# Layer-norm roots and inverses taken on four tokens per partition, and spread to the channels by TensorE

## The reference, cut to what matters

```python
def layer_norm(x, g, b):
    mu = jnp.mean(xf, axis=-1, keepdims=True)
    var = jnp.mean(jnp.square(xf - mu), axis=-1, keepdims=True)
    y = (xf - mu) * lax.rsqrt(var + EPS)
    return y * g + b

z = rms_norm(x, norm1_g) @ w_in          # 12 chunks of 128 columns
y_pool, s_pool = pool_mix(u_pool, ...)   # window means, then a 128x128 product per group
h = depthwise_conv(a * sigmoid(gate)) + conv_dw_b
y_conv = swish(layer_norm(h, ln_g, ln_b))
x = x + concat(y_pool, y_conv) @ w_out + b_out
x = x + hier_moe(rms_norm(x, norm2_g))   # 32 experts, top 2 of a group
```

## Time and profile before

| | us |
|---|---|
| median of 3 runs | 1005.97 |
| lowest and highest | 1005.02, 1008.71 |
| the profiled execution's own time | 1007.59 |
| its span | 1005.6 |
| PE busy in the span | 926.5 |
| DVE busy | 844.0 |
| ACT busy | 584.8 |

### The profile page before, as it was taken

One profiled execution on the slowest core, in us unless ns is written; L12 is line 12 of the kernel. 1 busy time (PEld: TensorE's weight loads), 2 busy tenths in 40 slices (PEclk: granted clock), 3 DMA queues, 4 the chain that ended last, 5 costly groups with the idle time before them and its releaser, 6 DMA issues.

```text
span 1005.6 us, 14019 instructions
## 1 busy us (share of the span) xinstructions
PE 926.5 (92%) x4691; PEld 791.8 (79%) x4691; DVE 844.0 (84%) x972; ACT 584.8 (58%) x560; POOL 165.1 (16%) x201
## 2 busy tenths in 40 slices
PE   5999999968999988999999999999999999999920
PEld 5999988857888787788888888888888888888710
DVE  6488997897678767989989899898989989898858
ACT  7311101385322254778878787887778778787514
POOL 1000000000000022242222222222212222221100
PEclk9999999999999979999999999999999999999965
DMA  9321241321332258899999999999999999999897
GB/s 284 114 64 42 66 130 54 135 88 63 137 114 105 95 193 320 315 388 386 379 396 369 387 382 381 397 374 398 391 390 387 391 399 375 399 390 382 325 310 273
DMA packets 66986, 275.69 MB, mean 274 GB/s; under 512 B 11615, under 2 KB 26591, under 8 KB 42377
## 3 DMA queue, kind: packets, MB, share of 16 engines
q1 hardware_dynamic: 57161, 257.41, 67.9%
q0 software_dynamic: 9792, 17.85, 4.7%
HBM read 259.33 MB, written 31.38 MB: 289 GB/s over the span
## 4 chain that ended last, share of the span: by engine, by line
PE 86%; DVE 7%; issue 2%; DMA 2%; ACT 2%; SPq 0%; POOLq 0%; POOL 0%; DVEq 0%; ACTq 0%
PE ps L1193 11%; PE ps L1195 11%; PE ps L1194 11%; PE ps L1212 6%; PE ps L1210 6%; PE ps L1211 6%; PE ps L924 5%; PE ps L925 5%; PE ps L926 5%; PE ps L968 3%; PE ps L1082 3%; PE ps L1083 3%; PE ps L1084 3%; PE ps L1165 3%; DVE big L1718 2%
## 5 line engine op out<-in xcount | busy, mean ns | idle before, releaser
L1718 DVE TENSOR_TENSOR big<-arena,big 128x2048 fp32r<-128x2048 f32 x128 | 286.9, 2283 | 0.0
L815 ACT ACTIVATE big<-arena 128x2048 fp32r<-128x2048 f32 x128 | 237.9, 1908 | 1.8 <-PE ps L1195 1.4
L1193 PE MATMUL ps<-big,ring 128*128 128x512 f32 x508 | 201.6, 397 | 2.8 <-DVE big L1718 2.8
L1195 PE MATMUL ps<-big,ring 128*128 128x512 f32 x508 | 198.7, 391 | 0.0
L1194 PE MATMUL ps<-big,ring 128*128 128x512 f32 x508 | 198.3, 390 | 0.0
L1718 DVE TENSOR_TENSOR slot_tail<-arena,slot_tail 128x2048 fp32r<-128x2048 f32 x62 | 139.0, 2283 | 0.0
L815 ACT ACTIVATE slot_tail<-arena 128x2048 fp32r<-128x2048 f32 x62 | 115.5, 1918 | 0.2 <-DVE eob L1694 0.2
L1193 PEld LDWEIGHTS ps<-big,ring 128*128 128x128 f32 x508 | 95.7, 188 | 22.3 <-DVE big L1718 3.7
L1195 PEld LDWEIGHTS ps<-big,ring 128*128 128x128 f32 x508 | 95.8, 188 | 20.5
L1194 PEld LDWEIGHTS ps<-big,ring 128*128 128x128 f32 x508 | 95.8, 189 | 18.9
L1210 PE MATMUL ps<-slot_tail,hTr 128*128 128x512 f32 x248 | 99.2, 400 | 0.0
(11 more groups left out here) (269 smaller groups left out, 1424.7 us busy)
## 6 DMA issues: line engine op xcount, KB each, us to landing
arena<-in_w_eg SPq DMA_DIRECT2D x64, 1024.0 KB, 7.8
arena<-in_w_eu SPq DMA_DIRECT2D x64, 1024.0 KB, 8.7
arena<-in_w_ed SPq DMA_DIRECT2D x64, 1024.0 KB, 9.2
arena<-in_x_prompt SPq DMA_DIRECT2D x16, 512.0 KB, 4.3
arena<-y_scratch SPq DMA_DIRECT2D x16, 512.0 KB, 8.2
arena<-in_w_in SPq DMA_DIRECT2D x12, 512.0 KB, 3.7
arena<-in_conv_band SPq DMA_DIRECT2D x8, 576.0 KB, 4.2
arena<-in_w_out SPq DMA_DIRECT2D x8, 512.0 KB, 5.2
```

The costliest lines, as they stand in the source:

```text
L815: act.activation(we_h[n % SLOTS], raw[n % RAWS], ACT.Copy).then_inc(high_done, 1)
L1193: pe.matmul(out, part_h[b][:, k, :], wh[:, i, :], start=(k == 0), stop=False)
L1195: ins = pe.matmul(out, part_l[b][:, k, :], wh[:, i, :], start=False, stop=(k == KD - 1))
L1718: dve.tensor_tensor(we_l[n % SLOTS], raw[n % RAWS], we_h[n % SLOTS].bitcast(F32), ALU.subtract).then_inc(low_done, 1)
```

## The change

For blocks 0 and 1 the variance, root and inverse are no longer held in 128 identical rows of 512 tokens, but as a 128x4 table: token q x 128 + p in partition p, column q.

- `ln_variance(n)`: four matmuls with the squares as the stationary operand and one column of `mean_w` as the moving one, instead of one matmul over 512 columns.
- `ln_deviation(n)`: a root over 128x4 into `stat_tok`. For n = 1 it waits for `lnrs_done` instead of `nrm_done`.
- A new `ln_inverse(n)` on DVE: a reciprocal over 128x4, a wait for it, and a product of the identity with the four inverses, which gives four 128x128 diagonals side by side (`diag`, 128x512).
- A new `ln_spread(n)` on PE: `ones` times `diag`, one matmul over 512 columns, which leaves the inverses in all partitions of PSUM bank 7. `ln_normal(n)` loses its reciprocal and multiplies from there.
- The engines' orders change: see the diff and the rows below. Block 2 keeps its form; its reciprocal has a function of its own, directly ahead of `ln_normal(2)`.

```diff
+        diag = r_p[:, 0:BANK].rearrange("p (q t) -> p q t", q=BANK // P)
+        tok_sd, tok_rs = stat_tok[:, 0:BANK // P], stat_tok[:, BANK // P:2 * BANK // P]
...
+        inv_ps = [banks(7, 1), banks(7, 1), None]
...
                 act.wait_ge(var_done, n + 1)
                 if n == 1:
-                    act.wait_ge(nrm_done, 1)
-                act.activation(ln_sd[n], var_ps[n][:, 0:w], ACT.Sqrt, bias=eps[:, :]).then_inc(lnsd_done, 1)
+                    act.wait_ge(lnrs_done, 1)
+                out = ln_sd[n] if n == 2 else tok_sd
+                act.activation(out, var_ps[n] if n < 2 else var_ps[n][:, 0:w], ACT.Sqrt, bias=eps[:, :]).then_inc(lnsd_done, 1)
...
             pooled(1)
-            ln_deviation(1)
+            state_rows(1)
             wo_high(0)
             pooled(2)
+            ln_deviation(1)
             ln_square(2)
             wo_high(1)
+            pooled(3)
             wo_high(2)
-            state_rows(1)
-            pooled(3)
             wo_high(3)
...
             def ln_variance(n):
                 w = BLOCKS[n][1]
                 pe.wait_ge(sqs_done, n + 1)
+                if n < 2:
+                    for q in range(w // P):
+                        ins = pe.matmul(var_ps[n][:, q:q + 1], sq[n][:, 0, q * P:(q + 1) * P], mean_w[:, 0:1], start=True,
+                                        stop=True)
+                    ins.then_inc(var_done, 1)
+                    return
...
+            def ln_spread(n):
+
+                pe.wait_ge(lnrs_done, n + 1)
+                pe.matmul(inv_ps[n], ones[:, :], diag.rearrange("p q t -> p (q t)"), start=True, stop=True).then_inc(inv_done, 1)
...
                     pool_lin_product(0)
-
+                    ln_spread(0)
+
+            pe.wait_ge(u_done, NG)
+            pe.wait_ge(nrm_done, 1)
+            turn_state(1)
             pool_lin_product(1)
-            pe.wait_ge(lnsd_done, 1)
+            pe.wait_ge(st_done, 2)
             ln_variance(1)
-            pe.wait_ge(u_done, NG)
             pool_lin_product(2)
             pe.wait_ge(cen_done, 2)
             ln_mean(2)
-            pe.wait_ge(lnsd_done, 2)
-            turn_state(1)
+            ln_spread(1)
             pool_lin_product(3)
...
+            def ln_inverse(n):
+                w = BLOCKS[n][1]
+                dve.wait_ge(lnsd_done, n + 1)
+                if n == 2:
+                    dve.reciprocal(ln_sd[n], ln_sd[n]).then_inc(lnrs_done, 1)
+                    return
+                dve.reciprocal(tok_rs, tok_sd).then_inc(inv_step, 1)
+                dve.wait_ge(inv_step, n + 1)
+                dve.tensor_tensor(diag, ident[:, :].unsqueeze(1).to_broadcast([P, w // P, P]),
+                                  tok_rs.unsqueeze(2).to_broadcast([P, w // P, P]), ALU.mult).then_inc(lnrs_done, 1)
...
             windows(2)
+            ln_inverse(0)
             ln_center(1)
             ln_normal(0)
             windows(1)
             ln_square_sum(1)
             windows(0)
+            ln_inverse(1)
             ln_center(2)
```

More of the change, by code:

```diff
@@ L162, in trunk_kernel @@
                     for i in range(len(PHASED))]
-        ln_sd = [r_p[:, 0:BANK], r_p[:, 0:BANK], r_p[:, BANK:BANK + DEC]]
+        stat_tok = sb("stat_tok", [P, 2 * BANK // P])
+        ln_sd = [None, None, r_p[:, BANK:BANK + DEC]]
+        diag = r_p[:, 0:BANK].rearrange("p (q t) -> p q t", q=BANK // P)
+        tok_sd, tok_rs = stat_tok[:, 0:BANK // P], stat_tok[:, BANK // P:2 * BANK // P]
         sq_at = BANK + DEC
@@ L270, in trunk_kernel @@
         mean_ps = [banks(6, 1), banks(6, 1), banks(6, 1)[:, 0:DEC]]
-        var_ps = [banks(7, 1), banks(7, 1), banks(6, 1)[:, DEC:2 * DEC]]
+        var_ps = [banks(7, 1)[:, 0:BANK // P], banks(7, 1)[:, 0:BANK // P], banks(6, 1)[:, DEC:2 * DEC]]
+        inv_ps = [banks(7, 1), banks(7, 1), None]
         out_ps = [banks(2, 2), banks(4, 2)]
@@ L324, in trunk_kernel @@
         cur_seen, placed = sem("cur_seen"), sem("placed")
+        inv_done, inv_step = sem("inv_done"), sem("inv_step")
         def x_rows(t):
@@ L1094, in turn_hm @@
                 else:
-                    pe.wait_ge(st_done, 2)
+                    pe.wait_ge(nrm_done, 2)
                     pe.wait_ge(lnsd_done, 3)
@@ L1433, in ln_center @@
                     [P, len(PHASED), w // PH, PH]), ALU.subtract).then_inc(cen_done, 1)
+            def ln_inverse(n):
[8 more added lines that the diff above has]
+                                  tok_rs.unsqueeze(2).to_broadcast([P, w // P, P]), ALU.mult).then_inc(lnrs_done, 1)
             def ln_normal(n):
                 w = BLOCKS[n][1]
-                dve.wait_ge(lnsd_done, n + 1)
-                dve.reciprocal(ln_sd[n], ln_sd[n]).then_inc(lnrs_done, 1)
-                dve.wait_ge(lnrs_done, n + 1)
+                inverse = ln_sd[n] if n == 2 else inv_ps[n]
+                if n == 2:
+                    dve.wait_ge(lnrs_done, n + 1)
+                else:
+                    dve.wait_ge(inv_done, n + 1)
                 dve.wait_ge(cen_done, n + 1)
                 tapped, phased = mixed(n)
-                dve.tensor_tensor(tapped, tapped, ln_sd[n].unsqueeze(1).to_broadcast([P, NTAP, w]), ALU.mult)
-                dve.tensor_tensor(phased, phased, by_phase(ln_sd[n]).unsqueeze(1).to_broadcast(
+                dve.tensor_tensor(tapped, tapped, inverse.unsqueeze(1).to_broadcast([P, NTAP, w]), ALU.mult)
+                dve.tensor_tensor(phased, phased, by_phase(inverse).unsqueeze(1).to_broadcast(
                     [P, len(PHASED), w // PH, PH]), ALU.mult).then_inc(nrm_done, 1)
@@ L1617, in _ @@
             ln_normal(1)
+            ln_inverse(2)
             ln_normal(2)
```

## The result

The changed kernel takes 1016.5 us, the median of 4 runs (1015.75 to 1020.76). Beside it the kernel before took 1006.43 us (4 runs, 1005.02 to 1008.71). The ratio is 1.0104, with an interval of 1.0074 to 1.0133: **slower by about 10 us**, with 1015.4 predicted. The profiled execution took 1016.42 us at a span of 1014.6, against 1007.6 and 1005.6 before, so the two profiles differ by 9.0 us and the medians by 10.1.

A forecast was written before the change was run, and what follows sets the result against it. The prediction took PE, 86% of the chain, as the bound, with the starts of chunk 11 and `out_proj(0)` deciding. 1.4 + 6.3 + 1.7 = 9.4 us on a median of 1005.97 gave 1015.4, range 1010.5 to 1019.0.

The forecast's parts named there:

- Chunk 11: Block 0: root, inverse and spread stand ahead of this chunk on PE, which starts at 200.1, 1.4 us later.
- The walk through block 1: Queues between 211 and 226: DVE waits 6.65 us for ACT's late root; delays `out_proj(0)` by 6.3 us.
- The clock: PE's 3.75 us idle gap puts the second spread and part of the last pooling product at 1.2 GHz: 1.7 us.
- Rival 1: Clock stays at 2.4 GHz after PE's gap: plus 7.7 us, 1013.7; chance 23%.
- `out_proj(0)` begins at half speed before and after, which cancels: At the start of `out_proj(0)`: the same low clock in both kernels, so no difference in time.
- the sum of 9.4: Whole kernel: 1.4 + 6.3 + 1.7 = 9.4 us slower, 1015.4 for the median.
- rival 3: `out_proj(0)` finds the clock high, giving back 2.5 us, perhaps another 1.5: 1010.5 to 1011.5; chance 8%.
- Rival 2: Clock also low under transposes and products behind two earlier PE gaps: some 5 us more, 1020.5; chance 6%.
- The table load: Ahead of block 1's root on ACT: 1.28 us load counted; about 1.4 us drain by the skill's rule left out.
- Rival 5: Broadcast operands as slow as the 3.34 us reciprocal: 2.65 us more in each block, 1020.7; chance 4%.
- Rival 4: DVE is the true limit, so the cheaper reciprocals save up to 4.9 us: 1001; chance 7%.
- What the second reciprocal gives back: nothing: `ln_normal(1)` loses 3.35 us, but ACT's Silus must wait for block 2's root behind `out_proj(0)`: no gain.

The follow-up runs named there:

- the old order: Changed kernel with ACT and PE in the order of the kernel before, the spread of block 1 behind the last pooling product: 1008.81 us.
- the earlier root: Changed kernel with one call moved: ACT takes the root of block 1 right behind the state's eviction: 1011.82 us.
- block 1 alone: Changed kernel with block 0 back in its old form, block 1 in the new form with the changed orders: 1016.89 us.
- the gap filled: Changed kernel plus 30 unused transposes of the identity on PE ahead of the second spread: 1016.48 us.
- the new order: The reordered kernel with its 28 transposes, block 1 in the new form, its spread inside `out_proj(0)`, block 0 in the old form: 1003.66 us.
- the repetition: The changed kernel run again, unaltered, beside other experiments: 1018.21 us, ratio 1.0124.
- the second set: A later group of experiments, measured against 1006.53 us for the kernel before (23 runs).
- the reordered kernel: Kernel before, arithmetic kept, block 1's variance moved into `out_proj(0)`, its root and work not needed for the first token tile behind `mix_high(0)`: 1008.16 us.

## Why the prediction was right, point by point

- **Chunk 11.** Forecast at 200.1, first matmul at 200.00, and it ends 1.4 us later once this execution's 0.2 us of later start are taken off. The variance of eight passes takes 0.81 us from start to start (195.31 to 196.12), so it was right to take no difference; root 0.26, reciprocal 0.18, diagonals 0.69. The spread waited 0.32 us instead of some 0.5.
- **The walk through block 1.** `pooled(1)` was forecast at 216.25 and came at 216.50. The root ended at 224.01 (223.7), DVE waited 6.86 us (6.65), PE idled 3.55 (3.75), the spread started at 225.01 (224.65). Every link is there and in its order, and of the two experiments that changed the order, the old order took away all of block 1's loss and the earlier root more than half, as the walk says.
- **The clock.** The low clock made spread and last product 0.84 + 0.96 = 1.8 us longer; I had taken 1.7. With it `out_proj(0)` was due at 235.4 and started at 235.94. Rival 1 (the clock stays high) is out for this profile.
- **What I had wrong: "`out_proj(0)` begins at half speed before and after, which cancels".** It was at half speed for some 3 us after the change and for 5 before, so 1.0 us came back there, and the profiled span grew by 9.0 and not 9.9. So the sum of 9.4 came as close as it did partly by luck: `out_proj(0)` started 0.5 us later than the sum has it, and the 1.0 us came off behind that. This is the mechanism of rival 3, at 1.0 us instead of 2.5 and more. It isn't a fixed term either: the length of `out_proj(0)` was 12.38, 13.90, 13.47, 13.06 and 12.42 us in the five profiles that hold block 1's changed order whole or nearly so.
- **Rival 2** (the clock is low under the earlier products too) happened in part: in block 1 alone and with the gap filled the product behind the variance lost 1.3 and 0.9 us to it. Of the changed kernel's eight runs the three longest, 1020.76, 1020.61 and 1019.35 us, had a mean granted clock of 0.963 to 0.965, and the two profiled ones (1016.42 and 1015.36 us) the highest, 0.968; at which products the long ones lost it isn't known, as none of them was profiled.
- **The table load.** The root begins 1.29 us after the load in the changed kernel too (222.46 to 223.75), directly behind an eviction. The Trainium skill (ScalarE: Activation LUTs, "What ACT_TABLE_LOAD costs") would add about 1.4 us of drain at the switch; this trace shows none here, as that of before did not.
- **Rival 5** (broadcast operands as slow as the reciprocal) is out: 0.69 us for the diagonals. **Rival 4** (DVE is the limit) is out as it stood: with no wait at DVE, in the old order, the time was 1008.81 and not 1001. It was half right in another sense: a full reciprocal becomes the limit as soon as `out_proj(0)` ends earlier.
- **"What the second reciprocal gives back: nothing"** holds in the old and in the changed order, for the reason given, though the old one has only 1.0 us between DVE's end of block 1 and the Silus. It fails in the new order.

What stays open: the last 1 to 3 us of the difference between medians (10.1, and 11.7 in the repetition) and profile (9.0, and 7.9 in the repetition, whose profiled execution was the fastest of its four). At the router's first product the two profiles of the changed kernel stand 8.9 and 8.8 us behind before, so what separates their spans lies behind that. The clock accounts for much of the rest: in every kernel here the longer runs tend to have the lower mean granted clock. In the second set the changed kernel took 1015.36 us at 0.968 and the kernel before a median of 1006.6 in its six runs at 0.968, 8.8 us less, while at 0.963 the changed kernel took 1019.35. No run here varies the clock by itself, so this is a correlation that fits, and not a cause shown.

## What to carry to other kernels

A cheaper instruction helps only where the dear one ended last, and the order that is made to fit it can cost more than it saves: here the new form of one block saved 3 to 4 us, changed nothing, or cost 8 to 9.5 us, with the same instructions in another order. Write the queues side by side and look for the first engine that would have to wait for a result made behind someone else's work; that wait, not the instruction, is the price. Before a step is made cheaper, shorten the path up to it and see whether it becomes the next bound, as the full reciprocal did.

## What the hardware showed that I had not expected

- **The clock falls at different places in the same work.** The product behind the second variance took 2.13 us in the changed kernel, 3.41 us in block 1 alone and 3.00 with the gap filled. PE's work and its gaps ahead of it, of 1.4 and 1.7 us, were the same in all three from chunk 11's end on. So the same gaps were followed by full clock in one execution and by half clock in another, and a stage can differ in length for it: `out_proj(0)` of the changed kernel by 1.5 us. What decides is not shown.
- **A filled gap kept the clock up, and it hardly showed in the time.** In the reordered kernel 28 transposes (3.23 us) cut `out_proj(0)` from 14.10 us (222.52 to 236.62) to 12.16 (222.54 to 234.70), while the medians, 1008.16 and 1007.46, cannot be told apart: the router's first product starts at 256.65 and 256.62, so the gain was gone by then. Stretches of the two kernels, first without and then with them (columns as above):

```profile
224.00:226.00 2.00, 2.00 (x6) 1.59 (x5) 2.00 (x3) 1.43 (x3) 0.00 (x0) 0.50 1.01 391
```

```profile
224.00:226.00 2.00, 2.00 (x10) 1.51 (x8) 2.00 (x3) 1.06 (x2) 0.00 (x0) 1.00 1.05 412
```

- **Eight passes over one column cost as much as two over 512.** The variance took 0.81 us from start to start in the new form and 0.86 in the old one, so the narrow form saves PE next to nothing.
